# A fixed first expert item, built from selection products, with its weights requested in the output projection and the item table computed on GpSimd

## What is computed

```
logits = h2 @ w_router + b_router
top_vals, top_idx = top_k(logits, 4);  gates = softmax(top_vals)
for each expert e, for the rows x of h2 that chose e:
    a = x @ w_up[e] + b_up[e]              # 1024 x 2048
    y = clamped_swiglu(a) @ w_down[e] + b_down[e]
    out[row] += gate[row, e] * y
```

## Time and profile before

| | |
|---|---|
| median of the runs | 1913.84 us |
| the profiled execution | 1913.18 us, of which the traced span is 1911.1 us |
| TensorE busy | 1836.1 us (96%), mean granted clock 0.986 |
| DVE busy | 1157.6 us (61%) |
| ACT busy | 884.4 us (46%) |
| Pool busy | 255.2 us (13%) |
| chain that ended last | TensorE 92%, DVE 3%, DMA 2% |
| HBM traffic | 270 GB/s over the span |

### The profile page before, as it was taken

The page is one execution under the profiler, slowest core; times in us unless marked ns, Lnnn a source line. Parts: engine busy times, 40 slices in busy tenths (PEclk is TensorE's granted clock), DMA queues, the critical chain, the costliest instruction groups (busy, mean ns, idle before and its releaser), DMA issues.

```text
span 1911.1 us, 33247 instructions
## 1 busy us (share of the span) xinstructions
PE 1836.1 (96%) x12118; PEld 1549.0 (81%) x12118; DVE 1157.6 (61%) x1695; ACT 884.4 (46%) x1212; POOL 255.2 (13%) x220
## 2 busy tenths in 40 slices
PE   7999998998699999999999999999999999999995
PEld 6777777787487888888888788888888889999884
DVE  5343376424799999999999844444444443434446
ACT  4312376423677767777777533333333232323224
POOL 0001000000212222221221201111011111111100
PEclk9999999999799999999999999999999999999998
DMA  5224791232899999999999978888888888878773
GB/s 199 73 83 138 195 249 46 87 120 90 332 407 378 362 351 379 360 362 375 368 375 353 366 251 287 287 288 287 283 282 283 285 289 290 279 257 278 257 252 149
DMA packets 176285, 507.98 MB, mean 266 GB/s; under 512 B 13732, under 2 KB 14372, under 8 KB 159774
## 3 DMA queue, kind: packets, MB, share of 16 engines
q1 hardware_dynamic: 158830, 456.85, 65.2%
q0 software_dynamic: 16272, 48.11, 8.9%
q10 hardware_dynamic: 1120, 2.16, 0.4%
HBM read 469.29 MB, written 46.33 MB: 270 GB/s over the span
## 4 chain that ended last, share of the span: by engine, by line
PE 92%; DVE 3%; DMA 2%; issue 1%; ACT 1%; DVEq 0%; POOL 0%; SPq 0%; ACTq 0%; POOLq 0%
PE ps L2124 26%; PE ps L2185 18%; PE ps L2266 6%; PE ps L2160 3%; PE ps L2273 3%; PE ps L2167 3%; PE ps L2134 3%; PE ps L2161 3%; PE ps L688 2%; PE ps L690 2%; PE ps L689 2%; PE ps L995 2%; PE ps L2010 2%; PE ps L1025 2%; PE ps L2106 2%; PE ps L2012 2%
## 5 line engine op out<-in xcount | busy, mean ns | idle before, releaser
L2124 PE MATMUL ps<-xg,weights 128*128 128x132 f32 (+4 forms) x4096 | 503.7, 285 | 2.5 <-DVE xg L1263 0.8
L2124 PEld LDWEIGHTS ps<-xg,weights 128*128 128x128 f32 x4096 | 497.5, 190 | 9.0 <-issue 9.0
L1867 DVE TENSOR_TENSOR weights_r<-weights,w_rounded 128x2048 fp32r<-128x2048 f32 x192 | 432.3, 2285 | 3.8 <-ACT w_rounded L1521 3.5
L1521 ACT ACTIVATE w_rounded<-weights 128x2048 fp32r<-128x2048 f32 x192 | 359.4, 1920 | 57.1 <-DVE weights_r L1867 30.0
L1395 POOL DMA_INDIRECT acc_d<-y_rows,row_index_now x62 | 111.3, 1796 | 802.6 <-ACT y_rows L1505 435.5
L1815 DVE TENSOR_TENSOR weights_r<-weights,w_down_rounded 128x1024 fp32r<-128x1024 f32 x128 | 148.1, 1219 | 28.9 <-PE ps L2138 28.9
L1371 POOL DMA_INDIRECT xg_rows<-h2g_d,row_index_next x64 | 107.1, 1674 | 336.0 <-DVE row_index_next L1798 202.2
L2185 PE MATMUL ps<-w_rounded,x_rounded 128*128 128x512 f32 x512 | 151.1, 397 | 0.0
L2185 PE MATMUL ps<-w_rounded,x_rest 128*128 128x512 f32 x512 | 148.5, 392 | 0.0
L1829 DVE TENSOR_SCALAR glu<-ps,b_up_t 128x132 f32<-128x132 f32 (+4 forms) x128 | 37.9, 358 | 174.2 <-PE ps L2124 174.2
L2185 PE MATMUL ps<-weights_r,x_rounded 128*128 128x512 f32 x512 | 129.9, 396 | 0.0
(11 more groups left out here) (318 smaller groups left out, 2863.2 us busy)
## 6 DMA issues: line engine op xcount, KB each, us to landing
weights<-in_w_up SPq DMA_DIRECT2D x128, 2048.0 KB, 10.2
weights<-in_w_down SPq DMA_DIRECT2D x64, 2048.0 KB, 15.2
weights<-in_w_in SPq DMA_DIRECT2D x3, 2048.0 KB, 8.7
xt<-in_x SPq DMA_DIRECT2D x8, 512.0 KB, 4.0
qk_d<-stage_rounded SPq DMA_DIRECT2D x16, 256.0 KB, 2.5
qk_d<-stage_rest SPq DMA_DIRECT2D x16, 256.0 KB, 2.9
q_stack<-qk_d SPq DMA_DIRECT2D x16, 256.0 KB
weights<-in_w_out SPq DMA_DIRECT2D x2, 2048.0 KB, 22.9
```

What stands on the lines that cost most here:

```text
L1521: ins = act.activation(wh[SLOT[j]][:], src, ACT.Copy)
L1867: ins = dve.tensor_tensor(piece_of(raw_r, j)[1], piece_of(raw, j)[1], wh[SLOT[j]][:].bitcast(F32), ALU.subtract)
L2124: last = pe.matmul(o, raw[c][:, k, t * P:(t + 1) * P], xg[:, k, 0:w], start=(k == 0), stop=(k == KT - 1))
```

## The change

Item 0 is no longer the first of the table. It is always expert `FIRST = 15`, with its first 128 rows; the table is made for what is left (128 rows are taken off the count of expert 15, items count from 1, and the loops of narrow items begin at 1).

- **Rows of item 0.** During the second half of the last output projection tile TensorE makes the positions of the first `EARLY = 6` tiles (21 small products) and an index product (6), DVE a selection of 768 columns and the index, and Pool gathers those rows (`first_rows`). The rows of tiles 6 and 7 are not gathered: 24 float32 matmuls (three for each of the 8 column blocks) add the transposed early rows and, through selection matrices, those of the late tiles, straight into the place where the transposed rows of an item are expected (`first_x`). A full index product follows for the scatter.
- **Weights of item 0.** SP asks for chunk 0 after the first half of the last projection tile, chunk 1 after the second half, the others after the early gather has landed. The buffers of the rounded pieces and of the bias table are laid out anew; ACT rounds pieces 0 and 1 right behind the projection.
- **Table.** The item table (41 instructions on Pool from the count on, 26 of them waited for by the next one), the sum of the gates and their scaling go from DVE and ACT to Pool. TensorE makes the two small products of the table inside item 0 (`class_sums`, `table_rows`). DVE copies a sum in between (after its second piece), waits after its fifth piece for the gates' sum (`Q_GATE`, behind the table in Pool's order), and reads the table after its eighth piece. SP asks for the weights of item 1, and Pool gathers the gates of item 0, behind that.
- **Bias tables** are rounded and subtracted between tiles of the output projection; the square root of the last tile comes before the copy of its transposed half.
- **Item 0 is written out** ahead of the loops on ACT, DVE and TensorE (`first`, `narrow(0, 1, first=True)`), with `class_ends` behind it. On TensorE the index product of item 1 comes before the first hidden transposes, and the transposes of its rows after the first half of the down products; on DVE the index of item 1 comes after piece 8.

```diff
+FIRST = 15
+EARLY = 6
...
-                with eng.Fori(0, last_narrow) as i:
+                with eng.Fori(1, last_narrow) as i:
...
-                sp.wait_ge(s_ex, 3)
+                for c in range(NCH):
+                    if c < 2:
+                        sp.wait_ge(s_og, 2 * NT - 1 + c)
+                    elif c == 2:
+                        sp.wait_ge(s_hs[0], 48)
+                    sp.dma_start(rows_of(raw[c], 2 if c < 4 else 4), narrow_chunk(FIRST, c)).then_inc(s_raw[c], 16)
+                sp.wait_ge(s_ex, 2)
                 sp.dma_start(h2g_d.rearrange("(i p) r -> p i r", p=P)[:, :, D:ROW], gall[:]).then_inc(s_gs, 16)
                 sp.wait_ge(s_tb, 1)
-                e0 = sp.value_load(tab[0:1, 0:1], min_val=0, max_val=NE - 1)
-                for c in range(NCH):
-                    if c == 1:
-                        n_items = sp.value_load(nit[0:1, NCLS - 1:NCLS], min_val=NE, max_val=MAX_ITEMS)
-                        last_narrow = sp.value_load(nit[0:1, NCLS + 1:], min_val=1, max_val=MAX_ITEMS)
-                        sp.wait_ge(s_rw[0], 16)
-                    sp.dma_start(rows_of(raw[c], 2 if c < 4 else 4), narrow_chunk(e0, c)).then_inc(s_raw[c], 16)
+                n_items = sp.value_load(nit[0:1, NCLS - 1:NCLS], min_val=NCLS + 1, max_val=MAX_ITEMS)
+                last_narrow = sp.value_load(nit[0:1, NCLS + 1:], min_val=1, max_val=MAX_ITEMS)
...
+                pool.tensor_scalar(taken, ecol[:, 0:1], float(FIRST), float(P), ALU.is_equal, ALU.mult).then_inc(s_dc, 1)
...
+                def done(ins):
+
+                    step[0] += 1
+                    ins.then_inc(s_dq, 1)
+                    pool.wait_ge(s_dq, step[0])
+
                 for i in range(NT):
+                    if i == NT - 1:
+                        pool.wait_ge(s_dv, N_INDEX)
+                        pool.wait_ge(s_gs, 16)
+                        for q in range(4):
+                            pool.wait_ge(s_hs[q], 32 if q + 4 < EARLY else 16)
+                        pool.reg_add(last_row, early_less_2, 1)
+                        pool.indirect_dma_start(out=first_rows[:], out_offset=None, in_=h2g_d[0:EARLY * P, :],
+                                                in_offset=bass.IndirectOffsetOnAxis(ap=first_index[:], axis=0),
+                                                bounds_check=last_row, oob_is_err=False).then_inc(s_hs[0], 16)
                     pool.wait_ge(s_x2, 2 * i + 2)
                     pool.dma_start(acc_d[i * P:(i + 1) * P, :], x2[i % 4][:]).then_inc(s_as[i % 4], 16)
+                    if i == NT - 1:
+                        done(pool.tensor_tensor(pmu[:], ident[:, 0:NE], ident[:, NE:2 * NE], ALU.add))
+                        done(pool.tensor_tensor(pme[:], ident[:, 2 * NE:3 * NE], ident[:, 3 * NE:], ALU.add))
+                        assert step[0] == Q_SELECTS
                     pool.wait_ge(s_h2, i + 1)
                     pool.dma_start(h2g_d[i * P:(i + 1) * P, 0:D], h2r[i % 4][:]).then_inc(s_hs[i % 4], 16)
+                    if i == EARLY - 1:
+                        for q in range(2):
+                            pool.wait_ge(s_as[q], 32)
+                        done(pool.memset(first_rows[:], 0.0))
+                        assert step[0] == Q_ROWS
+
+
+                items = ioi[0:NE, :]
+                count, over, rest = sm[:, 0:1], sm[:, 1:2], sm[:, 2:3]
+
+                done(pool.memset(gq[:, NFULL:], 0.0))
+                pool.wait_ge(s_dv, N_COUNT)
+                done(pool.tensor_scalar(hx[:, 0:1], count, 0.5, None, ALU.is_lt))
...
+                done(pool.tensor_tensor(cc[:], hx[:, 1:NCLS + 1], hx[:, 0:NCLS], ALU.subtract))
+                assert step[0] == Q_CLS
+
+
+                pool.wait_ge(s_dv, N_SUMS)
+                done(pool.tensor_scalar(cu[:], ccs[:, NCLS:], 1.0, None, ALU.max))
+                done(pool.tensor_scalar(cu[:, 0:1], cu[:, 0:1], 1.0, None, ALU.add))
...
+                done(pool.tensor_tensor(row2[:, 1, :], row2[:, 1, :], tsum[:], ALU.subtract))
+                assert step[0] == Q_ROW
+
+
+                pool.wait_ge(s_ex, 1)
+                done(pool.tensor_tensor(ex[:], ex[:], msk[:], ALU.mult))
+                done(pool.tensor_tensor(gall[:, :, 0:16], ex[:, :, 0:16], ex[:, :, 16:32], ALU.add))
+                for n in (8, 4, 2):
+                    done(pool.tensor_tensor(gall[:, :, 0:n], gall[:, :, 0:n], gall[:, :, n:2 * n], ALU.add))
+                done(pool.tensor_tensor(gsum[:, :, 0:1], gall[:, :, 0:1], gall[:, :, 1:2], ALU.add))
+                assert step[0] == Q_GATE
+                pool.wait_ge(s_gv, 1)
+                pool.tensor_tensor(gall[:], ex[:], gsum[:, :, 1:2].to_broadcast([P, NT, NE]), ALU.mult).then_inc(s_ex, 1)
                 for q in range(4):
                     pool.wait_ge(s_hs[q], 16 * NT // 4)
                     pool.wait_ge(s_as[q], 16 * NT // 4)
+                pool.wait_ge(s_gs, 32)
...
+                def first():
+
+                    act.wait_ge(s_og, 2 * NT)
+                    round_piece(0, 0)
+                    round_piece(0, 1)
+                    act.wait_ge(s_dq, Q_SELECTS)
+                    select_up(0, FIRST)
+                    x_narrow(0)
+                    act.wait_ge(s_rl, NT)
+                    act.wait_ge(s_gl, 1)
+                    round_piece(0, 2)
+                    act.activation(ex[:], ex[:], ACT.Exp).then_inc(s_ex, 1)
+                    for q in range(2, 4):
+                        act.wait_ge(s_hs[q], 32)
+                    act.wait_ge(s_bt, 1)
+                    for j in range(AHEAD + 1, U_PIECES + 1):
+                        round_piece(0, j)
+                        if j == AHEAD + 1:
+                            act.activation(s7[:], one[:], ACT.Sigmoid, scale=LIMIT * ALPHA)
+                    act.wait_ge(s_pd, 2)
...
+                    hidden_round(0, 1)
+                    act.wait_ge(s_tb, 1)
+                    select_up(1)
+                    x_narrow(1)
+                    for j in range(AHEAD):
+                        round_piece(1, j)
+                    y_narrow(0)
...
+                    if i == NT - 1:
+                        dve.wait_ge(s_dc, DISP_CONSTS)
+                        dve.wait_ge(s_as[1], 32)
+                        dve.wait_ge(s_dp, 1)
+                        first_position(early)
+                        told(first_select(first_hot[:, early, :], early, EARLY))
+                        assert step[0] == N_FIRST
+                        dve.wait_ge(s_dp, 2)
+                        done(dve.tensor_scalar(first_sum[:, 0:1], token[:, 0:1], float(BIGI), None, ALU.add))
+                        told(dve.tensor_tensor(first_index[:], first_sum[:, 0:1], token[:, 1:2], ALU.add))
+                        assert step[0] == N_INDEX
...
+                dve.wait_ge(s_dp, 4)
+                first_position(late)
+                told(first_select(first_sel[:], late, NT - EARLY))
+                assert step[0] == N_LATE
+                first_select(first_hot[:, late, :], late, NT - EARLY).then_inc(s_sel, 1)
+                dve.wait_ge(s_dp, 5)
+                told(dve.tensor_scalar(sm[:, 0:1], psum[1][0:NE, 8:9], taken, 0.0, ALU.subtract, ALU.max))
+                assert step[0] == N_COUNT
...
+                done(dve.scalar_tensor_tensor(out=pm, in0=psum[0][:, 0:NT * NE], scalar=1.0, in1=mk, op0=ALU.add, op1=ALU.mult))
+                assert step[0] == N_POS
+                dve.wait_ge(s_hs[1], 32)
+                dve.tensor_tensor(ex[:], lg[:], top8[:, :, 0:1].to_broadcast([P, NT, NE]), ALU.subtract).then_inc(s_gl, 1)
+
+                def item_table():
+                    dve.wait_ge(s_dp, 7)
+                    dve.tensor_copy(nit[:], cb[:])
+                    done(dve.tensor_copy(tab[:], psum[7][:, 256:256 + ITEMS]))
+                    done(dve.tensor_scalar(tbf[:], psum[7][:, 256 + ITEMS:256 + 2 * ITEMS], NOBODY + 1.0, None, ALU.add))
+                    dve.sem_inc(s_tb, 1)
...
+                def first():
+
+                    dve.sem_inc(s_pc, 2)
+                    dve.memset(ixn[:, 1:2], BIGI)
+                    index(0, 1, 7)
+                    dve.wait_ge(s_dp, 3)
+                    dve.tensor_copy(bup[:, 0:KT, :], psum[6][:, 0:KT * NE].rearrange("p (t e) -> p t e", t=KT))
+                    dve.tensor_scalar(bup[:, KT:, :], psum[6][:, KT * NE:].rearrange("p (t e) -> p t e", t=KT), 1.0, None, ALU.add)
+                    x_rest(0)
+                    for j in range(5):
+                        piece_rest(0, j)
+                        if j == 1:
+                            dve.wait_ge(s_dp, 6)
+                            told(dve.tensor_copy(ccs[:], psum[7][0:NE, 64:64 + 2 * NCLS]))
+                            assert step[0] == N_SUMS
+                    dve.wait_ge(s_dq, Q_GATE)
+                    dve.reciprocal(gsum[:, :, 1:2], gsum[:, :, 0:1]).then_inc(s_gv, 1)
+                    for j in range(5, U_PIECES):
```

(104 more changed lines are left out.)

357 lines of the change are left out of this document (166 added, 191 removed).

## The result

The changed kernel takes 1929.03 us (median of 4 runs, 1928.12 to 1931.16) where the kernel before takes 1913.83: ratio 1.0087, 95% interval 1.0074 to 1.0099. It is 15 us slower; 1915.4 was predicted and the range ended at 1923, so the measured time lies outside it. The profiled execution took 1929.71 us, its span 1928.0 (before: 1911.1).

The account below looks back on a forecast made before the run. TensorE, busy 96% of the span, bounds the kernel; gains lie in its waits behind the router. Terms: -16.4 (start), +14.7 (item 0), +3.0 (registers), +0.3 (early gather) = +1.6 on 1913.84, so 1915.4 us; range 1902 to 1923.

Parts of the forecast that it names:

- S + 54.8 + 3.0: Forecast start of item 1: item 0's start, its length of 54.8 us instead of 40.1, and 3.0 us of register loads.
- S = 481.9: Forecast start of item 0's first matmul, 16.4 us earlier than in the trace of the kernel before (498.27).
- the case that the prediction named at its end: Clock at half through the `first_x` matmuls before item 0, said to cost up to 2 us.
- Beside DVE, two steps in all: Pool's table beside pieces 2 to 4: about one waited step per subtraction, 0.4 us of the table's work.
- S + 12.3: Forecast end of DVE's piece 4 inside item 0, with 0.4 us lost to Pool.
- The chain, 8.5 us: Pool's table (6.5 us, 0.4 beside DVE) and six gate steps (2.4) before DVE's wait; bounds 4.5 to 17.
- Pool is dear: Rival: Pool's chain before DVE's `Q_GATE` wait costs more; at twice the price 8.5 us more, 1923.9; chance 0.19.
- From the chain's end to H, 12.4 us: Item 0 from 20.8 to H = 33.2: pieces 5 to 7, table copies, register load, `position_col`, selection, linear part, hidden rows.
- From the index to the rows, 10.2 us: Item 1's index out at 36.0, its gathered rows at 46.2; second block issued 3.4 us later, landing in 6.7 to 8.8.
- Half clock in item 0, 1.5 us: One stretch at half clock left in item 0, since TensorE idles 3 us of the 11 before it; 1.5 us.
- Registers, 3.0 us: Register loads between items 0 and 1: 4.6 us, about 1.6 hidden by the sequencer's lead; bounds 0 and 4.6.
- Behind item 1, 0: Narrow items after item 1: the forecast sum has no term for them.

Follow-up runs that it names:

- e10: e9 with the second weight chunk of item 0 asked for only after the early rows have landed; 1906.43 us, ratio 0.9966 to the kernel before.
- e1: Changed kernel with the item table back on DVE while TensorE makes item 0's rows, gates' sum still on Pool; 1916.14 us, ratio 1.0017 to the kernel before.
- e4: Changed kernel with 17 small scratch Pool instructions of four kinds behind the gathers of each narrow item; 1930.38 us in one execution.
- e2: Changed kernel with the table still on Pool but its class sums made and copied before item 0; 1922.38 us, ratio 1.0052 to the kernel before.
- e7: e6 with item 1's table, index and rows placed in item 0 where steady items have them; 1915.15 us, ratio 1.0011 to the kernel before.
- e3: Changed kernel with three of TensorE's waits in item 0 filled with products nobody reads; 1927.74 us, ratio 1.0075 to the kernel before.
- e6: e1 with DVE's start semaphores ahead of the table and the gates summed before item 0; 1912.0 us, ratio 0.9997 to the kernel before.
- e9: e7 with the gates' store issued on Pool's queue instead of SP's; 1906.57 us, ratio 0.9965 to the kernel before.

## Why the prediction was wrong

Item 1 was to start at 539.7 (S + 54.8 + 3.0); it started 13.6 us later. Step by step:

- **The start, S = 481.9: 485.4, +3.5.** That the gap closes was right. The early gather went out at 466.7, not at 465.5, and landed 9.4 us later, where the prediction took 8.8: +2.1. e10 shows that the 9.4 come of the two chunks beside it; for the issue, 0.9 us behind the index, nothing was tried. The 24 matmuls `first_x` took 7.15 us, not 5.4: the first three of the eight column blocks ran at half clock (granted 0.50 from 476 to 478, 1.00 from 480), the case that the prediction named at its end (up to 2 us) and left out of the sum. What follows them took 0.4 us less than its 2.6.
- **Beside DVE, two steps in all: none, +0.4, and piece 4 1.1 us later than S + 12.3.** The direction was right. The prediction's rule from the Trainium skill ("SBUF — State Buffer", section "Who interferes with whom"), that a GpSimd instruction which reads SBUF is blocked by a VectorE instruction with two SBUF inputs, agrees with the trace, which has 6.53 us for a step of 0.2. Not right was one step for each subtraction as a rule: e1, and e4 in part, show that, the changed kernel none in three and e2 one in five.
- **The chain, 8.5 us: 14.5, +5.6 beyond those 0.4.** This is the step that failed most, the largest term, and it lay within my bounds (4.5 to 17), between forecast and the rival "Pool is dear". The gates were right (2.5 against 2.4). The table took 11.8 us instead of 6.5: I had put unwaited steps at 0.1 to 0.15 us, by the memset and the iota of the earlier trace rows, and five of them with 64 columns and two scalars from SBUF took 0.57 each, and of six more of 64 columns with a scalar from SBUF five took 0.42 to 0.51 and one 0.31. By these rows an estimate puts some 3.9 us of the excess on these eleven steps. The plain ones of 64 columns with two inputs, at 0.31 and 0.08 for the semaphore, and the small ones, at 0.2 and 0.08, were each 0.05 to 0.1 over my price, 1.7 us in all by the same estimate. No row of before had a step with scalars from SBUF, and the memset, which reads nothing, was the wrong neighbour. The slope of 2.2 ns a column, an estimate from the figure for 2048 columns in the Trainium skill, "GPSIMD Engine Reference", section 3.1, is borne out: 0.31 us for 64 columns and 0.58 for 192 give 2.1. The fixed part of a step has no figure there.
- **From the chain's end to H, 12.4 us: 15.0, +2.6.** `position_col` took 2.58 us instead of 0.23, beside Pool's memsets: with Pool quiet in e7 it took 0.23 again. The piece after the reciprocal was stretched by 0.4 through the multiply of the gates. The prediction has no term for the memsets.
- **From the index to the rows, 10.2 us: 13.0, +2.8.** The gather's first block took 2.6 us beside the subtraction, its second went out 2.9 us behind it and landed 9.3 us later, where I had taken 6.8 and the earlier trace rows has 8.8. TensorE's waits were where I had put them: the table, the pieces, the hidden rest, the rows.
- **Half clock in item 0, 1.5 us: about 3 on the path.** 1.7 us at its start (part of it is the 1.1 of piece 4 above) and 1.4 behind the wait for the rows; the rest is hidden, as e3 shows.
- **Registers, 3.0 us: 0.8, -2.2.** The six loads take some 0.7 us each as in the earlier trace rows, but TensorE's sequencer was 4 us ahead and not 1.6 (the first began at 548.2, while the matmuls ran until 552.5). ACT begins its own only behind `y_narrow` (552.6 to 555.8); whether they cause the 0.55 us that item 1 takes beyond a steady one wasn't tried.
- **Behind item 1, 0: +2.3.** 15 items at 0.15 to 0.16 us each; the single longer items of both traces cancel. Not foreseen, and the cause not found.

Sum for the start of item 1, against 539.7: 3.5 + 0.4 + 1.1 + 5.6 + 2.6 + 2.8 - 2.2 = 13.8, less 0.2 from smaller terms (the index came 2.5 us behind H, not 2.8). The mechanism was the forecast one (the gap opens again inside item 0, in front of `Q_GATE`). The chain was priced at 8.5 us and took 14.5, and the weight of 0.19 for "Pool is dear" was too small: my price had been taken from the cheapest rows that Pool had.

But the chain alone would have given 1915.4 + 6.0 = 1921.4, inside the range, and even a chain of 17 us stood at 1923.9. Past 1923 the time went because the start, piece 4, `position_col`, the landing and the longer items were all dearer than forecast (12 us together), against 2.2 too much for the registers. The range had been drawn by moving the chain with all else held at the forecast.

What e6, e7 and e9 add: even without Pool's chain the change as written is worth nothing (e6), with the index of item 1 after DVE's eighth piece. Its gain (12.9 us at the start) is kept in part only when item 0 runs in the order of the steady items, and that needs the gates' store out of the weights' queue. The largest wait that e9 leaves TensorE in item 0 is 3.6 us for the selection of item 1, behind a `position_col` that lasts 2.52 us beside the same memsets; a kernel with the memsets elsewhere wasn't tried.

## What to carry to other kernels

Work that is moved to GpSimd to lie "beside" VectorE needs two prices: its own, by rows of the same form of instruction (inputs, scalars from SBUF, semaphore), and the time in which VectorE works with two inputs in SBUF, in which GpSimd's reads got at best one step in for each subtraction and here none in three. Before a chain is moved off an engine, look whether that engine has idle time elsewhere: here VectorE had 7.7 us of it in the shadow of TensorE's row products, and the table took 5.8 us there (1.3 more for the classes). And when a step is taken out of its place in a queue of DMAs, ask what lies ahead of it in bytes: 128 KB took 19.4 us behind the weights and 6.7 beside them.

## What the runs showed of the hardware that was not expected

- A GpSimd instruction that needs SBUF isn't always let in between two of VectorE's subtractions. Held over one: 2.2 to 2.4 us (e1, e4). Over two: 4.42 us (e2), and 2.9 to 3.0 us over a short one and a subtraction (e4). Over three: 6.53 and 6.75 us (changed kernel, e2). What decides is open.
- It goes the other way too: VectorE's `position_col` (8 columns) lasted 2.58 us beside GpSimd's memsets, and 0.23 without (e7). Subtractions of 128x2048 beside the same memsets were neither stretched nor did they hold them (kernel before: 4.49 us for two, 0.98 us for a memset).
- VectorE's instructions with an input from PSUM let GpSimd run at full speed (e4: 0.20 us a step beside `lin_rows`).
- An early gather of 128 rows lands 4.7 us after its issue with one weight chunk of 2 MB asked for before it (e10) and 9.3 to 10.4 us with two (the changed kernel and all made from it but e10).
